# Attention of three layers: the product with the values turned around, two heads per product

## The reference, cut to what matters

```
s = q @ k.T * scale + bias          # 128 queries x 256 to 640 keys
p = softmax(s)
o = p @ v                           # 128 x 64
y = concat(o over heads) @ w_out
```

## Time and profile before

| | |
|---|---|
| median of 3 runs | 3720.64 us (3718.24 to 3723.83) |
| profiled execution, its own time | 3717.82 us |
| its span, first to last instruction | 3716.0 us |
| PE busy | 3556.2 us, 96% |
| DVE / ACT / POOL busy | 2042.3 / 985.8 / 1208.4 us |
| attention of layer 0 | about 171 to 386 us of the span |
| attention of layer 2 | about 2138 to 2206 us |
| attention of layer 3 | about 3032 to 3097 us |

### The profile page before, as it was taken

One profiled execution on the slowest core, in us unless ns is written; L12 is line 12 of the kernel. 1 busy time (PEld: TensorE's weight loads), 2 busy tenths in 40 slices (PEclk: granted clock), 3 DMA queues, 4 the chain that ended last, 5 costly groups with the idle time before them and its releaser, 6 DMA issues. The chain is left out here.

```text
span 3716.0 us, 43381 instructions
## 1 busy us (share of the span) xinstructions
PE 3556.2 (96%) x15832; PEld 2599.1 (70%) x15832; DVE 2042.3 (55%) x3469; ACT 985.8 (27%) x2281; POOL 1208.4 (33%) x1175
## 2 busy tenths in 40 slices
PE   8999999999999998999999988899999998989999
PEld 5697555555555966688875556688885565668887
DVE  7575456544542175355555177478864448645654
ACT  2167121001120054211120164332212045422221
POOL 1000122222221032244440017556542005635554
PEclk9999999999999999999999998899999998899999
DMA  6300213333321100244442200134442210022222
GB/s 241 124 1 1 78 70 125 112 115 116 116 75 57 52 1 7 80 164 164 160 131 75 68 11 12 37 115 163 154 152 95 74 37 15 7 66 88 88 89 80
DMA packets 91088, 317.58 MB, mean 85 GB/s; under 512 B 10816, under 2 KB 13152, under 8 KB 90880
## 3 DMA queue, kind: packets, MB, share of 16 engines
q1 hardware_dynamic: 64224, 218.34, 18.1%
q10 hardware_dynamic: 24768, 90.19, 6.5%
q0 software_dynamic: 1888, 6.29, 0.6%
HBM read 312.68 MB, written 2.10 MB: 85 GB/s over the span
## 5 line engine op out<-in xcount | busy, mean ns | idle before, releaser
L1115 PE MATMUL ps<-arena 128*128 128x256 f32 (+1 forms) x3552 | 897.4, 406 | 3.4 <-DVE arena L1974 3.4
L1115 PEld LDWEIGHTS ps<-arena 128*128 128x128 f32 x3552 | 674.3, 190 | 193.1 <-issue 5.1
L609 PE MATMUL ps<-hbuf,ring 128*128 128x512 f32 (+1 forms) x1824 | 715.0, 555 | 8.6 <-ACT hbuf L1483 5.9
L609 PEld LDWEIGHTS ps<-hbuf,ring 128*128 128x128 f32 x1824 | 350.2, 193 | 368.5 <-issue 352.0
L2396 POOL TENSOR_TENSOR arena<-ring,arena 128x512 f32<-128x512 f32 (+1 forms) x132 | 169.8, 1287 | 801.6 <-PE ps L1115 801.6
L1115 PE MATMUL ps<-arena,ring 128*128 128x256 f32 (+1 forms) x1040 | 273.7, 406 | 2.0 <-ACT arena L1413 2.0
L1889 DVE CUSTOM_DVE_ANT_0 aring<-aring,csil,adab 128x1024 f32<-128x1024 f32 x176 | 268.6, 1547 | 1.7
L1115 PEld LDWEIGHTS ps<-arena,ring 128*128 128x128 f32 x1040 | 197.3, 190 | 57.6 <-ACT arena L1413 3.8
L913 PEld LDWEIGHTS ps<-arena 128*128 128x128 f32 x1440 | 174.9, 192 | 85.3 <-ACT arena L1308 61.2
L2379 POOL TENSOR_TENSOR arena<-ring 128x512 f32<-128x512 f32 (+1 forms) x132 | 169.7, 1286 | 165.2 <-PE ps L1115 163.5
L913 PE MATMUL ps<-arena 128*128 128x128 f32 x1440 | 204.6, 286 | 19.4 <-ACT arena L1322 11.9
(11 more groups left out here) (276 smaller groups left out, 5123.7 us busy)
## 6 DMA issues: line engine op xcount, KB each, us to landing
aring<-in_ada ACTq DMA_DIRECT2D x172, 512.0 KB, 4.7
ring<-in_mlp SPq DMA_DIRECT2D x128, 512.0 KB, 3.7
ring<-in_up SPq DMA_DIRECT2D x88, 512.0 KB, 3.3
ring<-in_in SPq DMA_DIRECT2D x56, 512.0 KB, 3.2
ring<-in_down SPq DMA_DIRECT2D x32, 512.0 KB, 3.5
ring<-in_odd_in SPq DMA_DIRECT2D x24, 512.0 KB, 3.2
arena<-in_ada SPq DMA_DIRECT2D x16, 512.0 KB, 13.7
ring<-in_out SPq DMA_DIRECT2D x16, 512.0 KB, 3.2
```

The lines of the kernel that those rows point to most:

```text
L609: mm = nc.tensor.matmul(slot[:, lo:hi], ring[:, c % RING, k, :], src[:, kt, lo:hi], start=kt == k0, stop=kt == k0 + nkt - 1)
L1115: mm = nc.tensor.matmul(ps[:, bank, 0:tw], w, x, start=start and j == 0, stop=j == len(pairs) - 1, skip_group_check=True)
```

## The change

For layers 0, 2 and 3 the operands of the last product change places. The values are stationary, and the turned probabilities of two items move as 256 columns. The output then has value columns on the partitions and queries along the row, 128 for each of the two items: of each item the half of the partitions that is its own is used. `turn_y` for the result is gone. The reciprocals, one number per query, have to be spread over the partitions: POOL writes each item's reciprocal 64 times into half of a 128x128 block, PE transposes this block, ACT copies it to SBUF (`take_inv`), and DVE multiplies the output by it, in two halves of 64 partitions, while writing `H` (`take_y`).

In layer 0 the items are put in another order, so that two successive items of one pair share a value block (head h and h + 4), there are four buffers for turned probabilities, and the rows of the weight blocks of `out0` are loaded in another order to match, as four DMAs per block.

```diff
@@ attention_items @@
-        return ([("a", h, n) for n in range(4) for h in range(8)] + [("b", h, m) for m in range(4) for h in range(8)]
-                + [("ca", h, n) for n in range(2) for h in range(8)] + [("cb", h, n) for n in range(2) for h in range(8)])
+        return [(kind, h + 4 * kv, n) for kind, tiles in (("a", 4), ("b", 4), ("ca", 2), ("cb", 2))
+                for n in range(tiles) for h in range(4) for kv in range(2)]
@@ SyncE: chunk @@
+                if name == "out0":
+                    for e in range(2):
+                        for odd in range(2):
+                            to = ring[64 * e:64 * e + 64, c % RING].rearrange("p (g i o) f -> p g i o f", g=2, o=2)[:, :, :, odd]
+                            rows_ = a[name][nb, 64 * odd:64 * odd + 64].rearrange("p (g e i) f -> p g e i f", g=2, e=2)[:, :, e]
+                            sp.dma_start(to, rows_).then_inc(w_arrived[c % RING], 16)
+                    return
@@ TensorE: attention @@
+                def pair_values(y):
+
+                    j = 2 * y + 1
+                    nt = key_tiles(vals[j])
+                    vt = pieces(layer, vals[j])[2]
+
+                    pe.wait_ge(inv_wide, wide_base(layer) + j + 1)
+                    if y >= 1:
+
+                        pe.wait_ge(yt_taken, ybase + y)
+                    nc.tensor.transpose(ps[:, Y_BANK, (y % 2) * P:(y % 2 + 1) * P], INVS[layer // 2][:, y % 2, :], ident[:, :]).then_inc(yt_ready, 1)
 
                     pe.wait_ge(pt_copied_act, vbase + j + 1)
                     if nt > 4:
                         pe.wait_ge(pt_copied_dve, p2 + seconds[j])
-                    if j >= 1:
-
-                        pe.wait_ge(y_ready, vbase + j)
                     for t in range(nt):
-                        mm = nc.tensor.matmul(ps[:, O_BANK, (j % 2) * P:(j % 2 + 1) * P], pt[:, j % 2, t * P:(t + 1) * P],
-                                              vt[t], start=t == 0, stop=t == nt - 1)
+                        mm = nc.tensor.matmul(ps[:, O_BANK, (y % 2) * 2 * P:(y % 2 + 1) * 2 * P], vt[t],
+                                              turned_pair(layer, y, t), start=t == 0, stop=t == nt - 1)
                     mm.then_inc(o_ready, 1)
...
                     if j < nv:
                         for i in range(per * j, per * j + per):
                             scores(i)
-                    if 2 <= j <= nv + 1:
-                        values(j - 2)
-                    if j >= 2 + per and j - 2 - per in ys:
-                        turn_y(ys[j - 2 - per])
+                    if layer == 1:
+                        if 2 <= j <= nv + 1:
+                            values(j - 2)
+                        if j >= 4:
+                            turn_y(j - 4)
+                    elif j >= 3 and j % 2:
+                        pair_values((j - 3) // 2)
                     if 1 <= j <= nv:
                         turn(j - 1)
@@ ScalarE: attention @@
-                def take_o(j):
...
+                def take_inv(y):
+                    act.wait_ge(yt_ready, ybase + y + 1)
+                    if y >= 2:
+
+                        act.wait_ge(yt_taken, ybase + y - 1)
+                    nc.scalar.activation((YT, YT2)[layer // 2][:, y % 2, :], ps[:, Y_BANK, (y % 2) * P:(y % 2 + 1) * P],
+                                         ACT.Copy).then_inc(inv_spread, 1)
...
                 for j in range(nv + 2):
...
-                    if j >= 2:
-                        take_o(j - 2)
+                    if j >= 3 and j % 2:
+                        take_inv((j - 3) // 2)
                     if 1 <= j <= nv:
                         copy_pt(j - 1)
                     if j < nv:
@@ VectorE: take_y @@
+                    dve.wait_ge(o_ready, ybase + y + 1)
+                    dve.wait_ge(inv_spread, ybase + y + 1 - len(value_items(1)) * (layer > 1))
+                    for hx in range(2):
+                        rows = slice(64 * hx, 64 * hx + 64)
+                        at = (2 * (y % 2) + hx) * P
+                        o, inv = ps[rows, O_BANK, at:at + P], (YT, YT2)[layer // 2][rows, y % 2, :]
+                        to = dst[rows]
                         if len(dst.shape) == 3:
-                            src = src.rearrange("p (r c) -> p r c", c=16)
-                        nc.vector.tensor_copy(dst, src).then_inc(yt_taken, 1)
+                            o, inv = (v.rearrange("p (r c) -> p r c", c=16) for v in (o, inv))
+                        x = nc.vector.tensor_tensor(to, o, inv, ALU.mult)
+                    x.then_inc(yt_taken, 1)
@@ GpSimd @@
+                elif kind == "attention" and layer != 1:
+                    for j in range(len(value_items(layer))):
+
+                        pool.wait_ge(inv_ready, att_base[layer] + j + 1)
+                        if j >= 4:
+
+                            pool.wait_ge(yt_ready, yt_base[layer] + j // 2 - 1)
+                        nc.gpsimd.tensor_copy(INVS[layer // 2][:, j // 2 % 2, 64 * (j % 2):64 * (j % 2) + 64],
+                                              small[:, 12 + j % 4:13 + j % 4].broadcast_to([P, 64])).then_inc(inv_wide, 1)
```

More of the change, by code:

```diff
@@ L720, in stretches @@
             return [(max(lo, a_), min(hi, b_), s_) for a_, b_, s_ in ranges(cols) if max(lo, a_) < min(hi, b_)]
+        ARRIVED = []
+        for c, (name, *_) in enumerate(CHUNKS):
+            ARRIVED.append((ARRIVED[c - RING] if c >= RING else 0) + 16 * (4 if name == "out0" else 1))
         CHUNK_OF = {}
@@ L795, in y_target, with wide_base, turned, turned_pair @@
             return H[:, 2 + h // 2, n * P:(n + 1) * P]
-        def buffers(layer):
-            return (PB, PT, YT) if layer < 2 else (PB2, PT2, YT2)
+        def wide_base(layer):
+            return val_base[layer] - (len(value_items(1)) if layer > 1 else 0)
+        def turned(layer, j):
+            if layer == 0:
+                return PT0[:, j % 4, :]
+            if layer == 1:
+                return PT[:, j % 2, :]
+            return (PT2, JUNK.rearrange("p (s t) -> p s t", s=2))[j // 2 % 2][:, j % 2, :]
+        def turned_pair(layer, y, t):
+            two = (PT0[:, 2 * (y % 2):2 * (y % 2) + 2] if layer == 0
+                   else (PT2, JUNK.rearrange("p (s t) -> p s t", s=2))[y % 2])
+            return two[:, :, t * P:(t + 1) * P]
         def pair_index(blk, d, hx, j):
@@ L903, in values @@
                     nt = key_tiles(vals[j])
-                    vt = pieces(layer, vals[j] if layer != 1 else vals[j])[2]
+                    vt = pieces(layer, vals[j])[2]
+                    pe.wait_ge(pt_copied_act, vbase + j + 1)
+                    pe.wait_ge(pt_copied_dve, p2 + seconds[j])
+                    if j >= 1:
+                        pe.wait_ge(y_ready, j)
+                    for t in range(nt):
+                        mm = nc.tensor.matmul(ps[:, O_BANK, (j % 2) * P:(j % 2 + 1) * P], turned(layer, j)[:, t * P:(t + 1) * P],
+                                              vt[t], start=t == 0, stop=t == nt - 1)
+                    mm.then_inc(o_ready, 1)
+                def pair_values(y):
+                    j = 2 * y + 1
+                    nt = key_tiles(vals[j])
+                    vt = pieces(layer, vals[j])[2]
+                    pe.wait_ge(inv_wide, wide_base(layer) + j + 1)
+                    if y >= 1:
+                        pe.wait_ge(yt_taken, ybase + y)
+                    nc.tensor.transpose(ps[:, Y_BANK, (y % 2) * P:(y % 2 + 1) * P], INVS[layer // 2][:, y % 2, :], ident[:, :]).then_inc(yt_ready, 1)
                     pe.wait_ge(pt_copied_act, vbase + j + 1)
@@ L1281, in attention @@
                 base, vbase, ybase = att_base[layer], val_base[layer], yt_base[layer]
-                pb, pt, yt = buffers(layer)
-                per = 2 if layer == 1 else 1
+                pb = PB if layer < 2 else PB2
                 def probs(i):
@@ L1304, in copy_pt @@
                     act.wait_ge(pt_ready, vbase + j + 1)
-                    if j >= 2:
-                        act.wait_ge(o_ready, vbase + j - 1)
-                    nc.scalar.activation(pt[:, j % 2, 0:n], ps[:, PT_BANK[0], 0:n], ACT.Copy).then_inc(pt_copied_act, 1)
+                    if layer == 1 and j >= 2:
+                        act.wait_ge(o_ready, ybase + j - 1)
+                    if layer != 1 and j >= 4:
+                        act.wait_ge(o_ready, ybase + j // 2 - 1)
+                    nc.scalar.activation(turned(layer, j)[:, 0:n], ps[:, PT_BANK[0], 0:n], ACT.Copy).then_inc(pt_copied_act, 1)
                 def square_o(j):
-                    act.wait_ge(o_ready, vbase + j + 1)
+                    act.wait_ge(o_ready, ybase + j + 1)
                     act.wait_ge(root_scale, j + 1)
@@ L1850, in attention @@
                     conv_center(layer - 2)
-                for j in range(nv + 2 + per):
+                for j in range(nv + (4 if layer == 1 else 2)):
                     if layer >= 2 and j in (1, 6, 7, 14, 15):
@@ L1869, in attention @@
```

(6 more changed lines are left out.)

60 lines of the change are left out of this document (29 added, 31 removed).

## The result

The changed kernel takes 3773.26 us (median of 4 runs, 3768.84 to 3778.2) against 3721.54 us before (4 runs): a ratio of 1.0137, 95% interval [1.0123, 1.0151], or 52 us more. Forecast was 3759 us with a range of 3738 to 3788. Two executions at a far lower mean granted clock (0.56 and 0.68; 6189.68 us of the kernel before and 5093.69 us of the ninth experiment's kernel, both in the last set of runs) are left out of every ratio.

What follows compares the result with a forecast made beforehand. PE, busy 96% of the span, was taken as the bound. Terms 7.4 + 5.2 + 6.9 + 3.2 + 14.0 + 1.6 = 38.3 us on 3717.8 gave 3756, with 2.8 for the median 3759 us, range 3738 to 3788.

Steps and rivals of the forecast that it cites:

- a POOL copy of 0.57 us: Wide reciprocals on POOL: at 0.57 the time is 3773 us; rival of a copy slower still, 13%.
- The order of work decides, +0.46 per pair of `b`: Odd item's turn waits for ACT's exponential behind a copy; pair 5.14 instead of 4.68 us, 7.4 us over 16 pairs.
- C: Start of ACT's copy of the even item's turned blocks, from which the prediction counts times within a pair.
- `a` with four blocks +0.65, with five +0.86, `ca` and `cb` +0.2: Added us per attention pair: 5.2 and 6.9 over 8 pairs each, 3.2 over 16 pairs of the last two kinds.
- `e` +0.70 with p = 0.35: PE's values wait for POOL's wide reciprocals, each copy taking p; 20 pairs at +0.70 us, 14.0 us.
- the lower of the two rows: Nearest profile rows for POOL's copy: 0.218 us (one operand, 128x1) and 0.567 (two operands, 64x128).
- an estimate of 0.32: POOL's copy time from the skill's best one-operand rate on the shortest row; sum would be about 1 us lower.
- The first two pairs of each layer are held by the convolution already: Kind `e`: these pairs were priced at nothing, leaving 20 of 24 pairs to pay.
- Bias preparations, 0.4 each: On DVE ahead of an even item's maximum, about two per layer, roughly 0.4 us each, 1.6 us in all.
- The product saves 0.24 per pair: PE's value product for a pair of four blocks: 1.72 us in one stream instead of 2 x 0.98.
- The rival in which PE's work decides: Exponential ready in time, only the shorter product counts: -0.24 us in 48 pairs, -15 us in all, 3705 us; 8%.
- `out0`'s loads cost nothing: Four DMAs per weight block: 11 us a block against a lead of about 10 us, first four during attention; no cost.

Runs made afterwards that it cites:

- ninth experiment: Kernel before, old product kept, both value products in the odd iteration, ACT and DVE reordered, bias preparations moved: 3723.04 us, ratio 1.0006.
- first experiment: Kernel before, with both items' value products in the odd iteration, old product and scaling kept: 3750.43 us, ratio 1.0081.
- second and fifth experiments: Both against the changed kernel: second, odd item's exponential before ACT's copy, 3761.83 us; fifth, POOL writes each wide reciprocal twice, 3790.16 us.
- third experiment: Changed kernel, with DVE's reciprocal of the odd item and copy of its fifth block before the next item's maximum: 3755.84 us, ratio 1.01.
- sixth experiment: Changed kernel, with four later bias preparations of layers 2 and 3 moved to odd iterations between reciprocal and take_y: 3774.3 us, ratio 1.0136.
- seventh experiment: Kernel before, with only layer 0's new item order and out0's weight blocks loaded by four DMAs each: 3723.3 us, ratio 1.0.
- eighth experiment: Changed kernel, with ACT's exponential and DVE's reciprocal moved first and bias preparations moved: 3711.35 us, ratio 0.9967; run again 3713.81 us, 0.9984.

## Why the prediction was right, and where its terms were off

The direction and its cause were right: the order of work, with ACT's exponential ahead of the turn and, in `e`, a reciprocal behind a maximum. The size was short: the sum was 38.3 us, the traces show 45.7 in the three stretches, and another 9.8 us of span lies outside them, where the prediction has nothing. Within layers 2 and 3 errors went both ways: the steady pairs of `e` were priced 3.7 us too high, their start and the bias preparations together 8.3 too low. That 3773 us is also what the prediction gives for a POOL copy of 0.57 us is chance: the copy took 0.24, and 0.36 beside a bias preparation of layer 0.

- **The order of work decides, +0.46 per pair of `b`.** Right: 0.48 (5.15 against 4.67), with turn at C + 1.32, copy at C + 2.01, values at C + 2.78 as worked out. The first experiment shows it by itself.
- **`a` with four blocks +0.65, with five +0.86, `ca` and `cb` +0.2.** Measured 0.74, 0.97 and 0.27. With four blocks, the pairs without a bias preparation take the 5.33 us of the forecast (4.68 + 0.65); the others take 0.08 more, because POOL's copy, which I took as hidden there, ends last and takes 0.36 us beside a preparation. With five blocks the values start at C + 3.76, where the forecast had 3.75, but not by DVE's copy alone: POOL's copy ends at 211.79 and DVE's at 211.88, and the ten records then take 2.24 us instead of 2.15.

```profile
211.28 0.41 DVE L2179 TENSOR_TENSOR arena<-arena 128x256 f32<-128x256 f32 x1
...
211.43 0.36 POOL L2560 COPY arena<-small 128x64 f32<-128x64 f32 x1 [3.95 <-DVE small L1863]
211.60 0.28 DVE L1887 COPY arena<-ps 128x128 f32<-128x128 f32 x1
...
212.03 2.40 PE L964 MATMUL ps<-arena 128*128 128x256 f32 x10
...
214.27 0.71 PE L931 MATMUL ps<-ident,arena 128*128 128x128 f32 x5
```

  For `ca` and `cb` the forecast had 3.10 before the change and 3.3 after, for both. `cb` was at 2.92, so its 3.19 is below the pitch forecast and still 0.27 above the old one. In layer 0 the sum was 22.7 us and the phase is 24.9 longer.
- **`e` +0.70 with p = 0.35.** Measured 0.57, because POOL's copy takes 0.24 us, near the lower of the two rows. The step (PE waits for POOL, POOL for a reciprocal behind a maximum) is right, as the second and fifth experiments show. The Trainium skill (GPSIMD Engine Reference, Elementwise) led to an estimate of 0.32; the row of 0.24 decides. The prediction also had GpSimd about half as fast by the Trainium skill (GPSIMD Engine Reference, Engine selection); the row there says so of operations with two inputs and calls one input, which this copy has, roughly line-rate. The term was 14.0 us for 20 pairs; 18 pairs at 0.57 are 10.3.
- **"The first two pairs of each layer are held by the convolution already" (nothing)** is a step that failed. From the second to the sixth copy it takes 15.8 us instead of 13.3, in both layers, 4.9 us in all. The third experiment, with the reciprocals first, has 14.5 there. So about half of it is the odd item's reciprocal waiting on DVE; what makes up the other half no experiment separates. The first step, before these, went from 3.91 to 5.43 us in layer 2 and from 6.29 to 5.41 in layer 3, which is not the change (last section).
- **Bias preparations, 0.4 each.** The term was mis-sized: 1.24 us for each of two pairs per layer, 5 us in all instead of 1.6. The sixth experiment takes it away locally, and the third as well. The timeline in the last section shows both parts of it.
- **The product saves 0.24 per pair.** The 1.72 us for eight new records was right (1.73). But the 2 x 0.98 on the other side holds for products with other work between them; two in a row take 1.78. Most of the saving comes from the pairing (0.18 of 0.23 us), and the pairing brings the wait. The rival in which PE's work decides comes near only once both orders are mended, with 4.50 us per pair of `b` where it would have 4.44.
- **`out0`'s loads cost nothing.** Right as far as 0.1% of the whole can tell, by the seventh experiment.

## What to carry to other kernels

When work of two items is merged into one step, every stream that used the time between the two steps loses its cover: look in each engine's order for what ran there, and move it before the merge. Locks in series hide each other, so one reordering alone shows little (10 and 16 us here) where both are worth 46. Price a product in the neighbourhood that it will have after the change, for its cost alone is not the cost beside others.

## What the runs showed of the hardware

**POOL's copy beside a DVE operation with two SBUF operands.** Its duration is 0.24 us at the median and 1.02 us at most. Timelines of layer 2 in the changed kernel:

```profile
2195.02 0.60 ACT L1363 ACTIVATE arena<-ps 128x512 f32<-128x512 f32 x1 [1.89 <-PE ps L931]
...
2195.20 1.09 DVE L2254 SCALAR_TENSOR_TENSOR arena<-arena 128x896 f32<-128x896 f32 x1
...
2196.33 0.70 DVE L1840 TENSOR_TENSOR ps<-ps,arena 128x512 f32<-128x512 f32 x1
...
2197.67 0.15 DVE L1863 RECIPROCAL small<-small 128x1 f32<-128x1 f32 x1
2197.74 1.07 DVE L2254 SCALAR_TENSOR_TENSOR arena<-arena 128x896 f32<-128x896 f32 x1
...
2197.88 1.02 POOL L2560 COPY arena<-small 128x64 f32<-128x64 f32 x1 [4.07 <-DVE small L1863]
```

POOL's copy starts while DVE reads 896 elements from two SBUF operands, and both end within 0.1 us of each other. Beside DVE's bias preparation of layer 0 (128x256, two SBUF operands, 0.41 us) it takes 0.36, and again ends 0.1 us after it. Beside DVE's work on PSUM, as in the rows of `b` and `e` above, it takes 0.24. The Trainium skill (GPSIMD Engine Reference, Key points) says that GpSimd shares its SBUF interfaces with VectorE and contends with its instructions of two SBUF inputs; the trace agrees, and gives the price here. The pair in these rows has the 1.24 us in two parts. DVE's bias add (L1840) starts 1.31 us after the copy (2195.02 to 2196.33) instead of 0.86, because a preparation stands ahead of it: 0.45. POOL's copy takes 1.02 instead of 0.24: 0.78. Together that is 1.23; no experiment takes the two apart.

**The granted clock elsewhere.** In the changed kernel's profile the turn at the start of layer 2's attention takes 1.12 us for four blocks where it took 0.66, and the four records of the convolution's variance product (L1070, L1017 before) 3.62 instead of 1.88 us. The windows view has a granted clock of 0.50 there (2174.7 to 2178.9), the 1.2 GHz level, against 1.00 before; PE had been idle for 3.1 us before, in both kernels. The change is not needed for it: in layer 3 of the kernel before the turn takes 1.11 and the product 3.62 too, at 0.50, and the eighth experiment's kernel has 3.62 in layer 2 and 1.88 in layer 3. So the first step between copies takes 5.5 us in one layer and 2.7 in the other of one and the same kernel. In the first 20 us after layer 1's last product the granted clock is 0.57 against 0.74 before, in work that the change does not touch. The seventh experiment's kernel, with every pitch as before, reaches layer 2's attention 7 us later than the kernel before does in its profile. So a good part of the 9.8 us of the span outside the three stretches is of the size that they vary by, and I don't put it down to the change. But it may not all be chance. The six profiles that have the new product and at least one of its two locks spend 3398 to 3404 us outside them; the seven others, from the kernel before (3390) to the experiments with the old product or with both locks mended, spend 3381 to 3395. Whether the waits in attention lower the clock of later work was not tested. Why a wait of the same length ends at the lower clock in one run and not in another stays open.
